# Scatter of an expert's rows as two float32r products with a one-hot matrix

## The chip, the cores and the metric

One core of a Trainium2 chip runs the whole program. The metric is the device time of one execution in microseconds (us); the time before is the median of three runs.

## The reference

The program computes two transformer blocks on 256 tokens of width 1024. The change touches only the second layer of the first block, a mixture of 8 experts (`moe_swiglu`). Each token goes to the 2 experts with the largest router logits, with softmax gates. Cut to what matters:

```python
top_logits, top_idx = lax.top_k(logits, TOP_K)        # 2 of 8
gates = jax.nn.softmax(top_logits, axis=-1)
...
h = jax.nn.silu(xb @ w1[e]) * (xb @ w3[e])            # 1024 -> 3584
y = h @ w2[e]                                         # 3584 -> 1024
y = y * gate_pad[:, None]
out = zeros.at[tok_pad].add(y)                        # back to the tokens' rows
```

## The kernel before

The experts run one after the other in a hardware loop (`turn`, once per expert, the last one outside the loop). At most 128 tokens of an expert are taken together (CAP = 128): a one-hot matrix gathers their rows, and another one scatters the result.

All weights are float32 in memory. Each 1 MB piece of weights (a slot, 128x2048) is loaded by two DMAs of 512 KB on the SP queue into a ring of 6 slots. ScalarE (ACT) copies it to float32r, the upper part (`weights_hi`, L1652), and VectorE (DVE) writes the rest as a second float32r tile (`weights_lo`, L1918). TensorE (PE) then forms a product as hi*hi + lo*hi + hi*lo, three float32r matmuls for each 128x512 block: L1158, L1159 and L1162 for w1 and w3 (`up_slot`), L1173, L1174 and L1178 for w2 (`down_slot`). A slot is 12 such matmuls, and a turn is 42 slots: 28 of "up" and 14 of "down". They run in the order up 1, down 0, up 2, down 1, up 3, down 2, next 0 (the first chunk of the next expert), down 3. At its slot s, the text of ACT and of DVE converts slot s + 3 first and then does the other work of slot s, so all work on an engine lies in the order of the text. A load may begin when PE has released the slot that stood in its place in the ring.

What surrounds the change, in the order of a turn:

- up 1, slot 4: `scatter(it, 0)` (L1141) writes the previous expert's rows for the first 128 tokens into PSUM banks 6 and 7, one matmul per bank of 512 columns. DVE adds both banks to `yacc` (`add`, L2271). Up 1, slot 6: `scatter(it, 1)` does the same for the other 128 tokens in the same banks, and so waits until both adds of the first part are done. The scatters of the last expert stand behind the loop. With 8 experts, there are 9 pairs, the first of them on zeros: 18 calls, 36 matmuls.
- down 1, slot 1: PE transposes `PG` (one-hot times gate, 128x256) into bank 6 (L1208), and ACT copies it to `PGT`, the stationary matrix of the scatter. PE waits for that copy at up 3, slot 1, where bank 6 is used again.
- down 3, slot 1, the last slot of a turn: ACT copies bank 4 and DVE copies bank 5 (L2318) to `Ysb`, the expert's 128x1024 result. ACT's copies of this kind all carry the line of a helper, L1466.
- at the head of the next turn, DVE does the lower part of the transposed activations (L2283), builds `PG` (`weigh`, L2256 to L2259) and the next gather matrix (`choose`, L2249 to L2252), converts four slots and then does the two adds of `scatter(it, 0)`.

Of the kernel before, what the change touches and what calls it, by code (L numbers as in the profile page):

```python
# [7 lines left out]
F32 = mybir.dt.float32  # L8
# [6 lines left out]
P = 128  # L15
# [15 lines left out]
CAP = P  # L31
# [218 lines left out]
def two_block_kernel(nc, a, out):  # L250

    CO, CONST_W = constant_offsets()
    with ExitStack() as ctx:
# [20 lines left out]
        def sem(name):  # L274

            if name not in S:
                S[name] = ctx.enter_context(nc.semaphore(name))
            return S[name]
# [111 lines left out]
        silu1 = ar(2, TT, FC)  # L390
        bufs1 = ffn_buffers(1, ar.at, silu1)
        ar.at += 3 * 4 * T
        Ysb = ar(D)
        Pm, PG, PGT = ar(TT, CAP), ar(TT, CAP), ar(TT, P)
        lo_slots = split_parts("weights_lo", "ring_data", 0, RING, 8 * FC)
        xT_hi, xT1_lo = split_parts("xT_hi", "actT", 0, DT, T), split_parts("xT_lo1", "arena", ar.at, DT, T)
        xg_hi, xg_lo = (split_parts(f"xg_{k}", "actT", D * i, DT, CAP) for i, k in enumerate(("hi", "lo")))
# [6 lines left out]
        fneg, fsum, frec = sm(H, TT), sm(H, TT), sm(H, TT)  # L404
        lgt, gtm, eqm = sm(TT, E), sm(TT, 64), sm(TT, 64)
        rank, sel, m1, ex, esum, gate = sm(TT, E), sm(TT, E), sm(TT), sm(TT, E), sm(TT), sm(TT, 2, E)
        posx, cnt, poscol, gcol = sm(TT, 2, E), sm(3), sm(TT), sm(TT)


        ring2 = Ring(ring_data, [sem(f"loaded2_{i}") for i in range(RING)], sem("weights2_used"), sem("weights2_hi"), sem("weights2_lo"), (2 * MIX_LOADS + FFN_LOADS) % RING)  # L410
# [394 lines left out]
        def _(pe):  # L805
# [308 lines left out]
            def moe():  # L1114
# [23 lines left out]
                def scatter(it, j):  # L1138

                    for q in range(2):  # L1140
                        mm(bank[6 + q][:, :], PGT[:, j, :], Ysb[:, 512 * q:512 * q + 512], start=True, stop=True).then_inc(sem("scatter_psum"), 1)  # L1141

                def turn_h(c):

# [36 lines left out]
                def turn(it, is_last):  # L1181
                    for s, (kind, c, m) in enumerate(Wide.slots(is_last)):
                        split = FFN_LOADS + e_first + s + 1 + it * MOE_LOADS
                        part = (kind, c, m)
                        if part in (("up", 1, 0), ("up", 2, 0), ("up", 3, 0), ("next", 0, 0)):

                            pe.wait_ge(sem("moe_h"), it * 4 + (c or 4))
                        if part == ("next", 0, 0):
                            pe.wait_ge(sem("xg_ready"), it + 2)
                        if part == ("up", 1, 1):  # L1190
                            turn_h(0)
                        if part == ("up", 1, 4):
                            pe.wait_ge(sem("ysb_ready"), it * 2 + 2)
                            pe.wait_ge(sem("pgT_ready"), it + 1)
                            pe.wait_ge(sem("moe_hT"), it * 4 + 1)
                            scatter(it, 0)
                        if part == ("up", 1, 6):
                            pe.wait_ge(sem("y_added"), it * 4 + 2)
                            scatter(it, 1)
                        if part == ("up", 2, 1):  # L1200
                            pe.wait_ge(sem("y_added"), it * 4 + 4)
                            turn_h(1)
                        if part == ("down", 1, 0):
                            pe.wait_ge(sem("moe_hT"), it * 4 + 2)
                        if part == ("down", 1, 1):
                            pe.wait_ge(sem("pg_ready"), it + 1)
                            for j in range(TT):
                                i = nc.tensor.transpose(bk(6, TT, P)[:, j], PG[:, j, :], ident)  # L1208
                            i.then_inc(sem("pgT_psum"), 1)
                        if part == ("up", 3, 1):  # L1210
                            pe.wait_ge(sem("pgT_ready"), it + 2)
                            turn_h(2)
                        if part == ("down", 2, 0):
                            pe.wait_ge(sem("moe_hT"), it * 4 + 3)
                            if not is_last:
                                gather(it + 1)
                        if part == ("next", 0, 1) or (is_last and part == ("down", 3, 0)):
                            if is_last:
                                pe.wait_ge(sem("moe_h"), it * 4 + 4)
                            turn_h(3)  # L1220
                        if part == ("down", 3, 0):
                            pe.wait_ge(sem("moe_hT"), it * 4 + 4)
                        (down_slot if kind == "down" else up_slot)(c, m, e_first + s, split)
# [240 lines left out]
        def _(act):  # L1464
            def a_(o, i, f, inc, **kw):
                nc.scalar.activation(o, i, f, **kw).then_inc(sem(inc), 1)  # L1466
# [187 lines left out]
            def moe():  # L1654
                act.wait_ge(sem("router_max"), 1)
                for j in range(TT):
                    a_(ex[:, j], lgt[:, j], ACT.Exp, "router_exp", bias=m1[:, j:j + 1])
                act.wait_ge(sem("npass_ready"), 1)
                last = act.value_load(npass_i[0:1, 1:2], min_val=E - 1, max_val=2 * E - 1)

                def gathered(it):
                    for b in range(2):
                        act.wait_ge(sem("gather_psum"), it * 2 + b + 1)
                        a_(xg_hi[:, 4 * b:4 * b + 4, :], bk(6 + b, 4, CAP), ACT.Copy, "xg_hi")

                def silu(c, used):
                    act.wait_ge(ring.used, used)
                    for q in range(Wide.WIDTHS[c] // 512):
                        i = nc.scalar.activation(esil[:, 512 * q:512 * q + 512], bank[q][:, :], ACT.Silu)
                    i.then_inc(sem("moe_silu"), 1)  # L1670

                def turned(c, n):
                    act.wait_ge(sem("moe_hT_psum"), n)
                    for b in range(Wide.WIDTHS[c] // 512):
                        i = nc.scalar.activation(ehT_hi[:, 4 * b:4 * b + 4, :], bk(6 + b, 4, P), ACT.Copy)
                    i.then_inc(sem("moe_hT_hi"), 1)

                def turn(it, is_last):
                    slots = Wide.slots(is_last)
                    n = len(slots)  # L1680
                    for s, (kind, c, m) in enumerate(slots):
                        if not is_last or s + Wide.LEAD < n:
                            e_high(e_first + s + Wide.LEAD, it)
                        used = n_moe + e_first + s + 1 + it * MOE_LOADS
                        part = (kind, c, m)
                        if part == ("up", 1, 0):
                            turned(0, it * 4 + 1)
                        if part == ("up", 2, 0):
                            turned(1, it * 4 + 2)
                        if part == ("down", 1, 1):  # L1690
                            act.wait_ge(sem("pgT_psum"), it + 1)
                            a_(PGT[:, :, :], bk(6, TT, P), ACT.Copy, "pgT_ready")
                        if part == ("up", 3, 0):
                            turned(2, it * 4 + 3)
                        if kind == "up" and m == Wide.UPS[c] - 1:
                            silu(c, used)
                            if c == 3 and not is_last:
                                gathered(it + 1)
                        if part == ("next", 0, 0) or (is_last and part == ("down", 2, 3)):
                            turned(3, it * 4 + 4)  # L1700
                        if part == ("next", 0, 7):
                            silu(0, used)
                        if part == ("down", 3, 1):
                            act.wait_ge(ring.used, used)
                            a_(Ysb[:, 0:512], bank[4][:, :], ACT.Copy, "ysb_ready")

                gathered(0)
                for m in range(2, e_first + Wide.LEAD):
                    if m == e_first + 1:
                        silu(0, n_moe + e_first)  # L1710
                    e_high(m)
                with act.Fori(0, last) as it:
                    turn(it, False)
                turn(last, True)
# [169 lines left out]
        def _(dve):  # L1884
# [316 lines left out]
            def moe():  # L2201
# [84 lines left out]
                def turn(it, is_last):  # L2286
                    slots = Wide.slots(is_last)
                    n = len(slots)
                    for s, (kind, c, m) in enumerate(slots):
# [23 lines left out]
                            turned_low(3, it * 4 + 4)  # L2313
                        if part == ("next", 0, 7):
                            multiply(0, it * 4 + 5)
                        if part == ("down", 3, 1):
                            dve.wait_ge(ring.used, n_moe + e_first + s + 1 + it * MOE_LOADS)
                            v.tensor_copy(Ysb[:, 512:1024], bank[5][:, :]).then_inc(sem("ysb_ready"), 1)  # L2318

                choose(0)  # L2320
                gathered(0)
                st.do(v.tensor_scalar(yacc[:, :, :], x[:, :, :], ALPHA, None, ALU.mult))

                v.memset(PGT[:, :, :], 0.0).then_inc(sem("pgT_ready"), 1)
                v.memset(Ysb[:, 0:512], 0.0).then_inc(sem("ysb_ready"), 1)
                v.memset(Ysb[:, 512:], 0.0).then_inc(sem("ysb_ready"), 1)
                st.settle()
                for m in range(2, e_first + Wide.LEAD):
                    if m == e_first + 1:
# [271 lines left out]
```

## Time and profile before

| | |
|---|---|
| three runs | 2479.80, 2483.47, 2486.38 us |
| median | 2483.47 us |
| span of the profiled execution, first to last instruction | 2475.4 us |
| busy: PE, DVE, ACT, POOL | 2313.0, 1569.0, 1140.9, 160.4 us |
| the expert loop with its ends, about 704 to 1738 us of the span | some 1034 us |
| one turn of the loop | 127.37 us |
| mean DMA rate over 740 to 1730 us | 345 GB/s |

The profiled execution has a span of 2475.4 us. Its own time is not listed apart; the median of the runs lies 8.1 us above the span and the lowest run 4.4 us, which is what lies around the span together with the spread between runs. Times in rows are us from the start of the span. PE's matmuls overlap in the records (each ends later than the next begins), so the distance from start to start tells what one costs.

### The profile page before, as it was taken

What the parts mean: (1) busy time and instruction counts of PE and PEld (TensorE: products, weight loads), DVE (VectorE), ACT (ScalarE), POOL (GpSimd) and SP (SyncE); (2) the same over time, 40 slices, a digit from 0 to 9 for tenths busy, and PEclk for the clock granted to TensorE, in tenths of its full rate; (3) what the DMA queues carried; (4) which work ended last, traced back from release to release, by engine and by line L of the source; (5) the groups of instructions that cost most, each with busy time, mean ns of one, the idle gap of its engine ahead of it and who ended that gap; (6) DMA issues with size and microseconds to landing.
All of it is one profiled execution on the core that took longest, in us unless ns stands there. A gap on an engine that the chain in (4) does not pass through costs nothing.

```text
span 2475.4 us, 31988 instructions
## 1 busy us (share of the span) xinstructions
PE 2313.0 (93%) x12191; PEld 1883.8 (76%) x12191; DVE 1569.0 (63%) x1677; ACT 1140.9 (46%) x1147; POOL 160.4 (6%) x224
## 2 busy tenths in 40 slices
PE   7987999798879999999999999999699999988997
PEld 6776788786767878787878787877588788756886
DVE  2565544365568888888898888887654219433443
ACT  1231443113246766667666666666544312222442
POOL 1010000102020000000000000000670001000000
PEclk9998999898889999999999999999899989788999
DMA  7402455450159999999999999999255444223552
GB/s 253 140 2 69 157 182 175 128 166 2 49 191 340 346 345 345 345 346 348 342 347 345 344 345 346 344 349 354 95 197 186 152 142 136 85 94 102 187 184 71
DMA packets 257660, 536.95 MB, mean 217 GB/s; under 512 B 20126, under 2 KB 150056, under 8 KB 257448
## 3 DMA queue, kind: packets, MB, share of 16 engines
q1 hardware_dynamic: 251088, 523.21, 60.1%
q0 software_dynamic: 3168, 9.86, 1.2%
q10 hardware_dynamic: 3320, 2.72, 0.3%
q8 instruction: 58, 0.95, 0.2%
q14 instruction: 26, 0.21, 0.0%
HBM read 532.57 MB, written 3.15 MB: 216 GB/s over the span
## 4 chain that ended last, share of the span: by engine, by line
PE 90%; DVE 5%; ACT 2%; issue 1%; ACTq 1%; DMA 0%; DVEq 0%; POOL 0%
PE bank L1159 8%; PE bank L1158 8%; PE bank L1162 8%; PE bank L1053 8%; PE bank L1054 8%; PE bank L1055 7%; PE bank L861 5%; PE bank L1292 4%; PE bank L1178 4%; PE bank L1173 4%; PE bank L1174 4%; PE bank L1030 2%; PE bank L857 1%; PE bank L1135 1%; PE bank L1141 1%
## 5 line engine op out<-in xcount | busy, mean ns | idle before, releaser
L1918 DVE TENSOR_TENSOR weights_lo<-ring_data,weights_hi 128x2048 fp32r<-128x2048 f32 x336 | 759.6, 2289 | 100.2 <-ACT weights_hi L1652 99.0
L1652 ACT ACTIVATE weights_hi<-ring_data 128x2048 fp32r<-128x2048 f32 x336 | 635.6, 1917 | 181.1 <-DMA ring_data<-in_moe_w 180.1
L1158 PE MATMUL bank<-weights_hi,xg_hi 128*128 128x512 f32 x896 | 363.4, 406 | 4.0 <-DVE arena L2277 2.6
L1159 PE MATMUL bank<-weights_hi,xg_lo 128*128 128x512 f32 x896 | 354.6, 396 | 0.0
L1913 DVE TENSOR_TENSOR weights_lo<-ring_data,weights_hi 128x2048 fp32r<-128x2048 f32 x99 | 229.7, 2348 | 51.7 <-ACT weights_hi L1491 51.7
L1466 ACT ACTIVATE arena<-bank 128x512 f32<-128x512 f32 (+4 forms) x178 | 83.6, 488 | 371.0 <-PE bank L861 111.8
L1162 PE MATMUL bank<-weights_lo,xg_hi 128*128 128x512 f32 x896 | 243.0, 393 | 0.0
L1053 PE MATMUL bank<-weights_hi,xT_hi 128*128 128x512 f32 x528 | 214.4, 406 | 16.3 <-issue 16.3
L1054 PE MATMUL bank<-weights_lo,xT_hi 128*128 128x512 f32 x528 | 210.9, 399 | 0.0
L1055 PE MATMUL bank<-weights_hi,xT_lo 128*128 128x512 f32 x528 | 210.6, 399 | 0.0
L1158 PEld LDWEIGHTS bank<-weights_hi,xg_hi 128*128 128x128 f32 x896 | 168.2, 188 | 46.1 <-issue 6.8
L1159 PEld LDWEIGHTS bank<-weights_hi,xg_lo 128*128 128x128 f32 x896 | 168.7, 188 | 42.0 <-issue 3.8
L1162 PEld LDWEIGHTS bank<-weights_lo,xg_hi 128*128 128x128 f32 x896 | 168.3, 188 | 40.2
L1491 ACT ACTIVATE weights_hi<-ring_data 128x2048 fp32r<-128x2048 f32 x99 | 185.7, 1917 | 0.0
L1173 PE MATMUL bank<-weights_hi,hT_hi 128*128 128x512 f32 x448 | 177.7, 397 | 1.5 <-DVE hT_lo L2283 1.5
L1174 PE MATMUL bank<-weights_hi,hT_lo 128*128 128x512 f32 x448 | 175.7, 392 | 0.0
L1930 DVE TENSOR_TENSOR hT_lo<-bank,hT_hi 128x256 fp32r<-128x256 f32 x66 | 25.0, 420 | 174.5 <-ACT hT_hi L1502 174.5
L861 PE MATMUL bank<-actT,ring_data 128*128 128x256 f32 x608 | 131.6, 379 | 0.0
L1053 PEld LDWEIGHTS bank<-weights_hi,xT_hi 128*128 128x128 f32 x528 | 101.0, 191 | 40.0 <-issue 17.4
L861 PEld LDWEIGHTS bank<-actT,ring_data 128*128 128x128 f32 x608 | 115.5, 190 | 15.6
L1502 ACT ACTIVATE hT_hi<-bank 128x256 fp32r<-128x256 f32 x66 | 21.7, 381 | 225.2 <-PE bank L1074 225.2
L1178 PE MATMUL bank<-weights_lo,hT_hi 128*128 128x512 f32 x448 | 123.1, 396 | 0.0
(432 smaller groups left out, 3261.0 us busy)
## 6 DMA issues: line engine op xcount, KB each, us to landing
ring_data<-in_moe_w SPq DMA_DIRECT2D x672, 512.0 KB, 4.2
ring_data<-in_ffn_w_in SPq DMA_DIRECT2D x88, 512.0 KB, 4.7
ring_data<-in_w_in SPq DMA_DIRECT2D x70, 512.0 KB, 4.7
ring_data<-in_ffn_w SPq DMA_DIRECT2D x66, 512.0 KB, 4.0
ring_data<-in_ffn_w_out SPq DMA_DIRECT2D x44, 512.0 KB, 3.9
ring_data<-in_w_out SPq DMA_DIRECT2D x24, 512.0 KB, 4.2
ring_data<-in_w_in SPq DMA_DIRECT2D x8, 396.0 KB, 4.0
ring_data<-in_w_in SPq DMA_DIRECT2D x8, 390.0 KB, 6.7
```

Source lines behind the costliest of these rows:

```text
L861: i = mm(bk(b, 2, T)[:, t], wt[:, k, P * t:P * t + P], actT[:, k, :], start=k == 0, stop=k == DT - 1)
L1053: mm(o, x_hi, w_hi, start=start, stop=False, **kw)
L1054: mm(o, x_hi, w_lo, start=False, stop=False, **kw)
L1055: return mm(o, x_lo, w_hi, start=False, stop=stop, **kw)
L1158: mm(o, xg_hi[:, k, :], e_hi(at)[:, r], start=k == 0, stop=False)
L1159: mm(o, xg_lo[:, k, :], e_hi(at)[:, r], start=False, stop=False)
L1162: i = mm(bank[2 * part + q][:, :], xg_hi[:, k, :], e_lo(at)[:, r], start=False, stop=k == DT - 1)
L1173: mm(o, ehT_hi[:, 2 * m + f, :], w_hi[:, f, cd], start=first and f == 0, stop=False)
L1174: mm(o, ehT_lo[:, 2 * m + f, :], w_hi[:, f, cd], start=False, stop=False)
L1652: nc.scalar.activation(e_hi(at), ring_data[:, e_slot(at), :], ACT.Copy).then_inc(ring.hi_done, 1)
L1913: v.tensor_tensor(f.lo_slot(f.n0 + at), w, f.hi_slot(f.n0 + at), ALU.subtract).then_inc(f.ring.lo_done, 1)
L1918: v.tensor_tensor(e_lo(at), ring_data[:, e_slot(at), :], e_hi(at), ALU.subtract).then_inc(ring.lo_done, 1)
```

## The change

The float32 matrix `PGT` (one-hot times gate) is split into a matrix of zeros and ones, `chosen` in float32r, and the gate of each of the 128 rows, `gslot`, which ACT gets as the row sum of its copy (`accum_out`). The gated result is held as two float32r parts: `Y_hi`, both halves by ACT straight from banks 4 and 5 with the gate as scale, and `Y_lo`, by DVE as bank*gate - `Y_hi`. Each scatter matmul becomes two, `chosen` times `Y_hi` and `chosen` times `Y_lo`, accumulated in one bank. DVE makes `chosen` with a comparison. PE has one more wait (`gslot_ready`), DVE waits for `y_hi`, and one of the memsets ahead of the loop is larger. The number of bytes loaded is the same.

```diff
 def scatter(it, j):
     for q in range(2):
-        mm(bank[6 + q][:, :], PGT[:, j, :], Ysb[:, 512 * q:512 * q + 512], start=True, stop=True).then_inc(sem("scatter_psum"), 1)
+        r = slice(512 * q, 512 * q + 512)
+        mm(bank[6 + q][:, :], chosen[:, j, :], Y_hi[:, r], start=True, stop=False)
+        mm(bank[6 + q][:, :], chosen[:, j, :], Y_lo[:, r], start=False, stop=True).then_inc(sem("scatter_psum"), 1)
...
 if part == ("up", 3, 1):                              # PE
     pe.wait_ge(sem("pgT_ready"), it + 2)
+    pe.wait_ge(sem("gslot_ready"), it + 1)
...
 if part == ("down", 1, 1):                            # ACT
     act.wait_ge(sem("pgT_psum"), it + 1)
-    a_(PGT[:, :, :], bk(6, TT, P), ACT.Copy, "pgT_ready")
+    a_(gate_row[:, :, :], bk(6, TT, P), ACT.Copy, "gslot_ready", accum_out=gslot[:, 0:1])
...
 if part == ("down", 3, 1):                            # ACT
     act.wait_ge(ring.used, used)
-    a_(Ysb[:, 0:512], bank[4][:, :], ACT.Copy, "ysb_ready")
+    act.wait_ge(sem("gslot_ready"), it + 1)
+    for q in range(2):
+        a_(Y_hi[:, 512 * q:512 * q + 512], bank[4 + q][:, :], ACT.Copy, "y_hi", scale=gslot[:, 0:1])
...
+if part == ("down", 1, 1):                            # DVE
+    dve.wait_ge(sem("gslot_ready"), it + 1)
+    v.tensor_scalar(chosen[:, :, :], gate_row[:, :, :], 0.0, None, ALU.is_gt).then_inc(sem("pgT_ready"), 1)
 if part == ("down", 3, 1):                            # DVE
-    dve.wait_ge(ring.used, n_moe + e_first + s + 1 + it * MOE_LOADS)
-    v.tensor_copy(Ysb[:, 512:1024], bank[5][:, :]).then_inc(sem("ysb_ready"), 1)
+    for q in range(2):
+        r = slice(512 * q, 512 * q + 512)
+        dve.wait_ge(sem("y_hi"), it * 2 + q + 1)
+        v.scalar_tensor_tensor(Y_lo[:, r], bank[4 + q][:, :], gslot[:, 0:1], Y_hi[:, r], ALU.mult, ALU.subtract).then_inc(sem("ysb_ready"), 1)
...
-v.memset(PGT[:, :, :], 0.0).then_inc(sem("pgT_ready"), 1)
-v.memset(Ysb[:, 0:512], 0.0).then_inc(sem("ysb_ready"), 1)
-v.memset(Ysb[:, 512:], 0.0).then_inc(sem("ysb_ready"), 1)
+v.memset(chosen.bitcast(F32)[:, :, :], 0.0).then_inc(sem("pgT_ready"), 1)
+v.memset(Y_hi.bitcast(F32)[:, :], 0.0).then_inc(sem("ysb_ready"), 1)
+v.memset(Y_lo.bitcast(F32)[:, :], 0.0).then_inc(sem("ysb_ready"), 1)
```

## Rows read from the trace of the kernel before

**Rows 1.** The page, busy time and share of the span by engine.
```profile
PE 2313.0 (93%) x12191; PEld 1883.8 (76%) x12191; DVE 1569.0 (63%) x1677; ACT 1140.9 (46%) x1147; POOL 160.4 (6%) x224
```
**Rows 2.** Busy time of each engine in a stretch of one turn.
```profile
core 0: us, PE busy (x) PEld busy (x) DVE busy (x) ACT busy (x) POOL busy (x), PEclk, DMA share, GB/s
...
880.00:1008.00 128.00, 128.00 (x578) 103.34 (x577) 109.85 (x71) 88.47 (x61) 0.00 (x0) 1.00 0.94 345
```
**Rows 3.** PE in order of time around a scatter: start, length, line.
```profile
1002.65 1.09 PE L1162 MATMUL bank<-weights_lo,xg_hi 128*128 128x512 f32 x4
1003.57 1.88 PE L1141 MATMUL bank<-arena 128*128 128x512 f32 x4
...
1005.52 0.39 PE L1159 MATMUL bank<-weights_hi,xg_lo 128*128 128x512 f32 x1
...
1010.85 1.88 PE L1141 MATMUL bank<-arena 128*128 128x512 f32 x4
```
**Rows 4.** All scatter matmuls: least, median and greatest ns.
```profile
L1141 PE MATMUL bank<-arena x72: 591/592/697, 748.4 to 1736.7; 128*128 128x512 f32 x72
```
**Rows 5.** DVE in order of time, from a turn's end to the adds.
```profile
993.52 0.68 DVE L2318 COPY arena<-bank 128x512 f32<-128x512 f32 x1
994.18 2.29 DVE L1918 TENSOR_TENSOR weights_lo<-ring_data,weights_hi 128x2048 fp32r<-128x2048 f32 x1
...
999.16 8.89 DVE L1918 TENSOR_TENSOR weights_lo<-ring_data,weights_hi 128x2048 fp32r<-128x2048 f32 x4
1007.97 1.28 DVE L2271 TENSOR_TENSOR arena<-arena,bank 128x512 f32<-128x512 f32 x2
...
1136.07 1.28 DVE L2271 TENSOR_TENSOR arena<-arena,bank 128x512 f32<-128x512 f32 x2
```
**Rows 6.** ACT in order of time at the same turn's end.
```profile
991.75 0.60 ACT L1466 ACTIVATE arena<-bank 128x512 f32<-128x512 f32 x1 [0.79 <-PE bank L1178]
992.24 1.91 ACT L1652 ACTIVATE weights_hi<-ring_data 128x2048 fp32r<-128x2048 f32 x1
```
**Rows 7.** Groups by shape whose operations are nearest to the new ones.
```profile
L1466 ACT ACTIVATE xT_hi<-bank,pcol 128x256 fp32r<-128x256 f32 x16 | 6.0, 489 | 7.0 <-PE bank L820 7.0
...
L1466 ACT ACTIVATE arena<-bank 128x256 f32<-128x256 f32 x17 | 6.3, 380 | 31.3 <-PE bank L861 18.3 <-PE bank L1288 10.0 <-PE bank L1292 3.0
...
L1906 DVE SCALAR_TENSOR_TENSOR xT_lo<-bank,pcol,xT_hi 128x256 fp32r<-128x256 f32 x16 | 6.5, 476 | 1.8 <-PE bank L820 1.8
...
L2547 DVE SCALAR_TENSOR_TENSOR x<-bank,x 128x512 f32<-128x512 f32 x8 | 5.0, 684 | 11.9 <-PE bank L1055 11.9
...
L2453 DVE TENSOR_SCALAR arena<-arena 128x384 f32<-128x384 f32 x1 | 0.4, 361 | 0.0
```
**Rows 8.** DVE behind the memsets, and PE at the first turn's second scatter.
```profile
727.52 2.29 DVE L1918 TENSOR_TENSOR weights_lo<-ring_data,weights_hi 128x2048 fp32r<-128x2048 f32 x1 [0.80 <-ACT weights_hi L1652]
...
756.01 1.98 PE L1141 MATMUL bank<-arena 128*128 128x512 f32 x4 [0.19 <-DVE arena L2271]
```
**Rows 9.** The last expert's scatters behind the loop, in order of time.
```profile
1731.81 0.69 DVE L2318 COPY arena<-bank 128x512 f32<-128x512 f32 x1 [6.00 <-PE bank L1178]
...
1732.56 1.99 PE L1141 MATMUL bank<-arena 128*128 128x512 f32 x4 [0.78 <-DVE arena L2318]
...
1733.72 0.69 DVE L2271 TENSOR_TENSOR arena<-arena,bank 128x512 f32<-128x512 f32 x1 [1.22 <-PE bank L1141]
...
1737.35 0.69 DVE L2271 TENSOR_TENSOR arena<-arena,bank 128x512 f32<-128x512 f32 x1 [0.17 <-PE bank L1141]
```
**Rows 10.** DMA over 740 to 1730 us in 40 slices; times to landing.
```profile
GB/s 291 350 387 305 373 332 345 371 305 369 348 337 363 314 363 360 330 359 328 349 369 319 362 361 319 360 321 371 353 317 374 310 370 360 315 368 319 362 375 333
...
DMA to landing us min/median/max: 3.1/4.2/6.3
```
**Rows 11.** What the DMA queue waited for, 880 to 1008 us.
```profile
SPq L595 <- PE bank L1162: 53.8, 28, 3.4
SPq L595 <- PE bank L1178: 27.7, 14, 5.3
```

More of the change, by code:

```diff
@@ L392, in two_block_kernel @@
         ar.at += 3 * 4 * T
-        Ysb = ar(D)
-        Pm, PG, PGT = ar(TT, CAP), ar(TT, CAP), ar(TT, P)
+        at_Y = ar.at
+        Y_hi = split_parts("Y_hi", "arena", ar.at, D)
+        Y_lo = split_parts("Y_lo", "cln", 0, D)
+        ar.at += D
+        Pm, PG, gate_row = ar(TT, CAP), ar(TT, CAP), ar(TT, P)
+        at_chosen = ar.at
+        chosen = split_parts("chosen", "arena", ar.at, TT, P)
+        ar.at += TT * P
         lo_slots = split_parts("weights_lo", "ring_data", 0, RING, 8 * FC)
@@ L406, in two_block_kernel @@
         rank, sel, m1, ex, esum, gate = sm(TT, E), sm(TT, E), sm(TT), sm(TT, E), sm(TT), sm(TT, 2, E)
-        posx, cnt, poscol, gcol = sm(TT, 2, E), sm(3), sm(TT), sm(TT)
+        posx, cnt, poscol, gcol, gslot = sm(TT, 2, E), sm(3), sm(TT), sm(TT), sm(1)
         ring2 = Ring(ring_data, [sem(f"loaded2_{i}") for i in range(RING)], sem("weights2_used"), sem("weights2_hi"), sem("weights2_lo"), (2 * MIX_LOADS + FFN_LOADS) % RING)
```

## The prediction

> **What bounds the kernel now.** I read the page first. PE is busy for 2313.0 of 2475.4 us, and no other engine comes near [rows 1]. The share is a mean over stages, so the next view is that of the expert loop alone, where the change lies. In a stretch of one turn PE is busy for 128.00 of 128.00 us at the full granted clock (2.4 GHz), DVE for 109.85 and ACT for 88.47 [rows 2]. The reader should see that there is no gap at all on PE: what PE is spared here shortens the turn, as long as nobody else comes too late. Two others could. DVE is at 86%, and the DMA engines at 94% [rows 2]. So I then read the timeline of DVE and ACT where the change adds work to them, and the DMA views. The DMA queue itself spends 53.8 + 27.7 = 81.5 of 128 us waiting for PE to release a slot [rows 11]: loads follow PE, they do not lead it.
>
> **The scatter on PE.** Before, one call is 2 float32 products. The trace keeps two records for each (72 for 36) [rows 4]. From the first start to the next product with weights is 1005.52 - 1003.57 = 1.95 us, and one float32r product (the L1158 that lies between) must come off. Four float32r products take 1003.57 - 1002.65 = 0.92 us, so one is 0.23 and the call is 1.72 us [rows 3]. After, one call is 4 float32r products with weights loaded for each, just what L1162 does: 0.92 to 0.93 us. A call gets 1.72 - 0.93 = 0.79 us shorter, and the 18 calls, all on the path, would give 14.2 us. That is the upper bound; now the calls are taken one kind at a time.
>
> **The seven later turns.** Two calls each: 2 x 0.79 = 1.58 us, 11.1 us for seven, if nothing waits. The place where something could wait is `scatter(it, 1)`, which needs both adds of `scatter(it, 0)`. DVE ends these adds at 1007.97 + 1.28 = 1009.25, and PE starts the call at 1010.85 [rows 3, 5]: 1.60 us of slack. The change eats it from both ends. First, PE comes 0.79 us earlier because `scatter(it, 0)` is shorter. Second, DVE comes later. Its copy L2318 (0.68) becomes two operations that read a bank, a column and a tile. The nearest rows are the same operation on 128x256 with a column (476 ns, 6.5 / 16 = 0.41 us of busy time each) and on 128x512 with a constant (684 ns) [rows 7]. A 128x512 one with a column should be 0.69 to 0.75, the pair 1.41, so DVE is 0.73 us later. From 994.18 DVE works almost without a gap up to the adds, four conversions in 8.89 us among it [rows 5], so nothing there absorbs the delay. What is left is 1.60 - 0.79 - 0.73 = 0.08 us. It is just enough on paper; with 0.1 us of error in each term I allow a mean wait of 0.1 us in each turn, 0.7 us in all. In one turn the adds start at 1136.07, 0.73 us later than 1007.97 + 127.37 = 1135.34 [rows 5], because ACT's conversion came late; there the new DVE work falls into DVE's idle time, and the slack is again about 0.08.
>
> DVE must not wait for ACT before `Y_lo`. ACT starts its copy at 991.75, when the bank is complete [rows 6]. A 128x512 copy takes 0.60 there; a scale column costs 489 - 380 = 109 ns more on 128x256 [rows 7], so 0.71, and two of them end by about 991.75 + 1.3 = 993.05. DVE reaches this point at 993.52 [rows 5], later, so it does not wait. ACT's next conversion moves from 992.24 to 992.9 and ends at 994.8; DVE needs it after its own two operations, at 993.52 + 1.41 = 994.93. This hides the ACT part too, by 0.1 us only. If that cover is gone, each tenth goes to the same 0.08 us of slack.
>
> **The other edits in a turn.** `chosen` is a comparison on 128x256 from SBUF; the nearest row is 361 ns on 128x384 [rows 7], so about 0.3 us. It stands behind a conversion in the middle of the turn, four slots (4 x 12 x 0.23, 11 us) before PE asks for it, and DVE has 128 - 110 = 18 us of idle time in the turn, none of it needed by PE [rows 2]. The row sum adds a short read to ACT's copy in the same place; even at a whole extra copy (0.38 us, [rows 7]) it is under the same cover. PE's extra wait is for something done long before. I put all three at nothing, with an upper bound of 0.7 us on the two engines but not on PE.
>
> **The first turn and the memsets.** Here `scatter(0, 1)` starts at 756.01 after waiting 0.19 us for DVE's adds [rows 8]. DVE is itself late at this point, so a faster `scatter(0, 0)` only makes PE wait 0.98 instead of 0.19: gain 0. The second call still gives 0.79. The larger memset costs DVE about 1 us, but DVE waits for ACT 0.80 us at 727.52 [rows 8] and stands idle again after that conversion. Nothing.
>
> **Behind the loop.** Now the change is a chain with no cover. Before: bank complete at 1731.81, copy 0.69, PE at 1732.56, first add at 1733.72 (1.16 later), last add ends at 1737.35 + 0.69 = 1738.04: 6.23 us [rows 9]. After: first `Y_hi` 0.71, second by 1.3, then DVE's two from 0.75 to 2.16, PE at 2.2. The first sum is ready one product earlier than before: a pair takes 0.46 where the float32 product took 0.86, so 1.16 becomes 0.76. Then two adds, 1.35, and the second call repeats both: 2.2 + 2 x (0.76 + 1.35 + 0.05) = 6.5 us. A loss of 0.3 us, between 0 and 0.6.
>
> **The sum.** 11.1 - 0.7 + 0.8 - 0.3 = 10.9, say 11 us. All later stages begin after the loop and move with it; their loads are issued as slots come free. The span would be 2475.4 - 11 = 2464.4 us. The median of the runs is 8.1 us above the span, and I carry the difference over: 2483.5 - 11 = 2472.5 us. Bounds: 14 if every call counted; 5.5 if the whole gain of `scatter(it, 0)` were lost to DVE in seven turns.
>
> **DMA against a rule.** A turn loads 42 x 1.049 = 44.0 MB, now at 345 GB/s; in 125.8 us it would be 350 GB/s. One slice of 24.75 us already shows 387 GB/s, several over 370 [rows 10], so the trace leaves room. The Trainium skill, "HBM Reference", Specifications, gives an effective 358 GB/s per core, and in Access says a core alone streams well above it. By the 358 a turn could not be shorter than 44.0 / 0.358 = 123 us, still under 125.8, and the sum would be the same; the slices over 358 side with its second statement.
>
> **Rivals.**
>
> *A, as above: PE sets the turn.* 2472.5 us. For it: no gap on PE. Range of its own 2469 to 2476. Chance 0.68.
>
> *B, DVE comes too late for `scatter(it, 1)`.* The slack of 0.08 us is small against the sum of three estimates. If DVE is 0.8 us later than I think, seven turns lose 5.6 us and the gain is 5.3: 2478 us. It needs a slower column operation or a wait for the second `Y_hi`; against it speak the rows of the same operation. Chance 0.15.
>
> *C, the loads cannot come faster.* If 345 GB/s is all that this pattern yields, PE will wait for weights what it is spared: 2483 us. For it: the share of 94% in the turn. Against: the queue's 81.5 us of waiting for PE, and slices of 370 to 387 GB/s; time to landing is at most 6.3 us where PE takes 5 x 2.79 = 14 us to come round to the slot. Chance 0.09.
>
> *D, slower.* `Y_hi` stands on ACT behind a conversion that waits for its load, and DVE now waits for ACT before it may go on, which it did not before. If that load is late by L, DVE's conversions and the adds are late by L less the cover: 0.79 us of idle ACT [rows 6], 0.47 between 993.05 and 993.52, 0.08 of slack. Each us beyond 1.3 costs a us in each of seven turns. At L = 2.9 the gain of 11 is gone; at L = 4.5 the kernel is at about 2483.5 - 11 + 7 x 3.2 = 2495 us. The greatest landing time is only 2.1 us above the median [rows 10], so it would have to be a new kind of lateness. Chance 0.04. The remaining 0.04 is for more than 14 us of gain, from a change of the loads' timing that I do not see.
>
> **How the numbers follow.** The bound between a change and none is 0.3%, 7.5 us, about the spread of these runs: 2476.0 is where "faster" begins. A lies 3.5 us beyond it. A and the rest of 0.04 make 0.72; I leave a little of A to "same" for the spread of a median of three. Same: B, C and that, 0.26. Slower: D, 0.04. The range reaches from 2467 (14 us of gain and some spread) to 2481 (B and some spread), and leaves out C and D.
>
> **What the profile after would show.** L1141's successor as four float32r products in 0.93 us; turns of 127.37 - 1.58 = 125.8 us, plus what PE waits at `scatter(it, 1)`; the adds of `scatter(it, 0)` ending 5.68 + 0.73 = 6.4 us after its start (now 1009.25 - 1003.57 = 5.68); DVE's idle time before `Y_lo` near 0 with ACT as releaser only behind the loop; the DMA rate in a turn at 350 GB/s. PE idle time with DVE's add as its releaser, 0.5 us or more in each turn, would speak for B; idle time with `weights_hi` or `weights_lo` for C; DVE idle before `Y_lo` for D. The prediction is wrong if a float32r product that follows another on the same bank costs more than 0.23 us, or if DVE's gapless run in front of the adds is longer than I count.

## The result

| | median | runs | span of the profiled execution |
|---|---|---|---|
| before | 2481.64 us | 2478.05 to 2486.38, 4 runs | 2475.4 us |
| after | 2465.75 us | 2462.36 to 2469.73, 4 runs | 2466.9 us |

The ratio of the runs is 0.9940, with a 95% interval from 0.9924 to 0.9955: the kernel became faster, by 0.45 to 0.76%. The forecast was 2472.5 us with a range from 2467 to 2481. The direction was right; the measured median lies 1.25 us below the range.

The two profiled executions differ by only 8.5 us, although the medians differ by 15.9. The four runs after took 2469.73, 2464.70, 2466.80 and 2462.36 us, and the profiled one is the slowest of them, with a span of 2466.9: only 2.8 us lie around the span. This disagreement between profile and clock is the first thing to be explained; the second is whether the steps of the sum were right.

### The profile page after: what moved, and what is told of

It is laid out like the page before. It is cut to its first block, busy times and chain, and to the rows that moved or that the text cites. A ratio compares the mean times of both kernels' runs of the same rounds, so it can differ in the third digit from the quotient of the medians.

```text
span 2466.9 us, 32044 instructions
## 1 busy us (share of the span) xinstructions
PE 2303.1 (93%) x12191; PEld 1886.1 (76%) x12191; DVE 1575.4 (64%) x1693; ACT 1147.8 (47%) x1163; POOL 160.3 (6%) x224
## 4 chain that ended last, share of the span: by engine, by line
PE 89%; DVE 6%; ACT 2%; issue 2%; ACTq 1%; DMA 1%; DVEq 0%; POOL 0%; SPq 0%
PE bank L1167 8%; PE bank L1166 8%; PE bank L1170 8%; PE bank L1059 8%; PE bank L1060 8%; PE bank L1061 8%; PE bank L867 5%; PE bank L1301 4%; PE bank L1186 4%; PE bank L1181 4%; PE bank L1182 4%; PE bank L1036 2%; PE bank L863 1%; PE bank L1141 1%; PE bank L1449 1%
## 5 line engine op out<-in xcount | busy, mean ns | idle before, releaser
L1166 PE MATMUL bank<-weights_hi,xg_hi 128*128 128x512 f32 x896 | 357.0, 398 | 4.0 <-DVE arena L2288 2.6
```

What stands on the lines that cost most here:

```text
L1166: mm(o, xg_hi[:, k, :], e_hi(at)[:, r], start=k == 0, stop=False)
```

## The profile after

The page and a window of two turns, as in [rows 1] and [rows 2]:

```profile
PE 2303.1 (93%) x12191; PEld 1886.1 (76%) x12191; DVE 1575.4 (64%) x1693; ACT 1147.8 (47%) x1163; POOL 160.3 (6%) x224
```

```profile
877.28:1003.04 125.76, 125.76 (x575) 102.78 (x574) 109.93 (x72) 89.07 (x63) 0.00 (x0) 1.00 0.96 350
1003.04:1128.82 125.78, 125.78 (x576) 102.74 (x574) 110.12 (x72) 89.21 (x63) 0.00 (x0) 1.00 0.95 350
```

These stretches reach from one `scatter(it, 0)` to the next. A turn is 125.76 us, where it was 127.37: 1.61 us less, forecast 1.58. PE is still busy without a gap at the full clock, and the DMA rate is 350 GB/s, as worked out. The Trainium skill's 358 GB/s for a core ("HBM Reference", Specifications) bound nothing here; the turn stays below it, and single slices had gone over it already [rows 10]. The Trainium skill's sentence on a core that streams alone, which the prediction puts under Access, stands under Specifications as well.

PE and DVE in order of time around the scatter, to set beside [rows 3] and [rows 5]:

```profile
1002.81 0.40 PE L1170 MATMUL bank<-weights_lo,xg_hi 128*128 128x512 f32 x1
1003.04 0.39 PE L1148 MATMUL bank<-Y_hi,chosen 128*128 128x512 f32 x1
1003.27 0.39 PE L1149 MATMUL bank<-Y_lo,chosen 128*128 128x512 f32 x1
1003.50 0.39 PE L1148 MATMUL bank<-Y_hi,chosen 128*128 128x512 f32 x1
1003.73 0.39 PE L1149 MATMUL bank<-Y_lo,chosen 128*128 128x512 f32 x1
1003.96 0.40 PE L1166 MATMUL bank<-weights_hi,xg_hi 128*128 128x512 f32 x1
...
1009.54 0.40 PE L1148 MATMUL bank<-Y_hi,chosen 128*128 128x512 f32 x1
```

```profile
993.00 1.40 DVE L2334 SCALAR_TENSOR_TENSOR Y_lo<-bank,small,Y_hi 128x512 fp32r<-128x512 f32 x2
994.42 2.29 DVE L1929 TENSOR_TENSOR weights_lo<-ring_data,weights_hi 128x2048 fp32r<-128x2048 f32 x1
...
999.25 8.89 DVE L1929 TENSOR_TENSOR weights_lo<-ring_data,weights_hi 128x2048 fp32r<-128x2048 f32 x4
1008.06 1.28 DVE L2282 TENSOR_TENSOR arena<-arena,bank 128x512 f32<-128x512 f32 x2
```

A call is 1003.96 - 1003.04 = 0.92 us, four products 0.23 apart, where it was 1.72. DVE enters `Y_lo` without idle time, and its adds end at 1008.06 + 1.28 = 1009.34. PE comes back at 1009.54. The slack of 1.60 us has shrunk to 0.20 (forecast 0.08): present, and nearly used up. PE came 0.78 us earlier, counted from the first call (6.50 us instead of 7.28), and DVE's adds started 0.62 us later (5.02 us after the first call instead of 4.40), where 0.73 had been forecast.

The new operations by shape, beside [rows 7]:

```profile
L2334 DVE SCALAR_TENSOR_TENSOR Y_lo<-bank,small,Y_hi 128x512 fp32r<-128x512 f32 x16 | 11.2, 745 | 6.7 <-ACT Y_hi L1475 6.7
...
L1475 ACT ACTIVATE Y_hi<-bank,small 128x512 fp32r<-128x512 f32 x16 | 10.1, 685 | 12.6 <-PE bank L1186 12.6
...
L2329 DVE TENSOR_SCALAR chosen<-arena 128x256 fp32r<-128x256 f32 x8 | 2.3, 286 | 0.0
```

All three fall where the nearest rows had put them (0.69 to 0.75, 0.71 and 0.3 us). DVE waits for `Y_hi` 6.7 us in all, and that is the wait behind the loop alone, where ACT itself waits as long for PE's last bank.

Two places stand apart from these turns. At the first turn's second call PE waits for DVE, 0.97 us where 0.98 had been forecast:

```profile
757.91 0.50 PE L1148 MATMUL bank<-Y_hi,chosen 128*128 128x512 f32 x1 [0.97 <-DVE arena L2282]
```

Behind the loop it went otherwise than in the sum. Beside [rows 9], all engines in order of time:

```profile
1721.63 1.27 ACT L1475 ACTIVATE Y_hi<-bank,small 128x512 fp32r<-128x512 f32 x2 [6.73 <-PE bank L1186]
1722.35 1.41 DVE L2334 SCALAR_TENSOR_TENSOR Y_lo<-bank,small,Y_hi 128x512 fp32r<-128x512 f32 x2 [6.72 <-ACT Y_hi L1475]
...
1723.82 0.80 PE L1148 MATMUL bank<-Y_hi,chosen 128*128 128x512 f32 x1 [2.22 <-DVE Y_lo L2334]
1724.41 0.63 PE L1149 MATMUL bank<-Y_lo,chosen 128*128 128x512 f32 x1
1724.83 0.63 PE L1148 MATMUL bank<-Y_hi,chosen 128*128 128x512 f32 x1
...
1728.79 0.69 DVE L2282 TENSOR_TENSOR arena<-arena,bank 128x512 f32<-128x512 f32 x1 [0.17 <-PE bank L1149]
```

From the last bank complete (ACT starts at 1721.63) to the end of the last add (1728.79 + 0.69 = 1729.48) are 7.85 us. It was 6.23; the forecast was 6.5. The copies end as worked out: PE starts 2.19 us after the bank is complete, forecast 2.2. But the products then stand 0.42 us apart and not 0.23. The windows give the clock that PE was granted there, first after, then at the second call behind the loop in the kernel before:

```profile
1718.00:1721.00 3.00, 3.00 (x15) 2.42 (x14) 0.00 (x0) 0.00 (x0) 0.00 (x0) 1.00 1.09 350
1721.00:1724.00 3.00, 0.78 (x4) 0.34 (x3) 1.41 (x2) 2.37 (x3) 0.00 (x0) 0.92 0.99 349
1724.00:1726.00 2.00, 1.89 (x4) 0.98 (x4) 0.76 (x2) 2.00 (x2) 0.00 (x0) 0.50 1.05 349
```

```profile
1734.60:1738.00 3.40, 2.18 (x5) 0.81 (x5) 2.01 (x3) 2.69 (x2) 0.00 (x0) 1.00 0.59 201
```

A granted clock of 0.50 is 1.2 GHz, where 1.00 is 2.4.

To compare the loop between executions, I use the time from the first scatter's first record to the end of the last add. Before it is 748.37 to 1738.04, 989.67 us; after it is 750.28 to 1729.48, 979.20 us. So the loop with its ends gained 10.5 us, and the stages ahead of it took 1.9 us more in this one profile. The rest, behind the last add, is 737.4 us in both.

## The experiments

### Both kernels again

No edit; both kernels were timed and profiled again.

> The changed kernel as it is, timed again. Theory 1 (all of the gain lies in the expert loop): between the first scatter and the last add the profiles show 989.67 us before and 979.20 after, so 10.5 us, and the rest of the 15.9 us between the medians is the spread of the runs: ratio 0.9958, 10 to 12 us. Theory 2 (the stages ahead of the loop gain too): 15 us again, ratio 0.994, and a profile in which the loop begins earlier than at 748.37 us, the place before. In both the turns take 125.76 us.

> The kernel before, timed against itself, as a measure of the spread. Theory 1: ratio 1.000 with an interval of some 0.001 to each side; single runs 2478 to 2487 us, and the first scatter starts within 2 us of 748.37 us while turns take 127.37 us again. Theory 2: the start of the loop is the same within 0.5 us in each profile of this kernel.

The changed kernel took 2469.28 us (2465.61 to 2471.72, 6 runs) and is at 0.9955 of the kernel before (0.9941 to 0.9969), 11.2 us; the medians are 12.8 us apart (2482.08 before, 23 runs). The kernel before against itself is at 0.9998 (0.9987 to 1.0009), with a median of 2480.91; its single runs reach from 2474.27 to 2487.67, further down than the 2478 expected. PE of the changed kernel and of the kernel before, in order of time, first call and the same call a turn later:

```profile
749.25 0.39 PE L1148 MATMUL bank<-Y_hi,chosen 128*128 128x512 f32 x1
...
755.74 0.39 PE L1148 MATMUL bank<-Y_hi,chosen 128*128 128x512 f32 x1
...
875.01 0.39 PE L1148 MATMUL bank<-Y_hi,chosen 128*128 128x512 f32 x1
```

```profile
752.31 1.88 PE L1141 MATMUL bank<-arena 128*128 128x512 f32 x4
...
879.69 1.88 PE L1141 MATMUL bank<-arena 128*128 128x512 f32 x4
```

The kernel before began its loop at 748.37 in one execution and at 752.31 in the other, so theory 2's condition (the same within 0.5 us) fell, and so did theory 1's (within 2 us). Over all eleven profiles of this study the start lies between 747.02 and 754.87 us, in kernels whose work ahead of the loop is the same but for the memsets, and without order by kernel. (Two memsets are larger in the changed kernel, not one: 0.91 us each instead of 0.48.) Behind the last add come 736.6 to 741.7 us. The loop itself repeats: 989.67 and 989.20 us before, 979.20 and 977.62 after. The difference of 1.6 between the last two comes from the first turn (127.00 and 125.76 us), where PE waited 0.97 us in the first profile and not at all in this one (755.74), and from the end (7.85 and 7.55 us).

So the loop gains between 10.0 and 12.1 us, the second timing agrees, and over the eleven profiles the start of the loop moves by some 8 us and the stretch behind it by some 5, whatever the kernel. The first comparison, with four runs to a side, showed 15.9 us between medians, and its interval begins at 11.2.

The kept traces say something on where the start of the loop is lost. A window of 25 us ahead of it, in the second profile of the changed kernel (loop from 749.25) and of the kernel before (from 752.31):

```profile
125.00:150.00 25.00, 22.02 (x108) 16.12 (x106) 18.58 (x25) 10.10 (x32) 0.00 (x0) 0.90 0.00 1
125.00:150.00 25.00, 22.38 (x93) 15.92 (x91) 18.17 (x24) 7.51 (x29) 0.00 (x0) 0.80 0.00 0
```

In the seven profiles whose loop begins before 751 us the granted clock is 0.90 to 1.00 here, and ACT reaches its table load at the end of this stretch at 147.86 to 148.78. In the four that begin after 752 it is 0.80 or 0.67, and the same table load comes at 150.48 to 153.41. No weights are loaded in this window, so the loads are not behind it. The table load is late by 1.7 to 5.5 us, the start of the loop by 2.0 to 7.9. The clock and the lateness go together; no run changed one of them, so that the clock is the cause is not shown.

### New parts, old product

```diff
-mm(bank[6 + q][:, :], chosen[:, j, :], Y_hi[:, r], start=True, stop=False)
-mm(bank[6 + q][:, :], chosen[:, j, :], Y_lo[:, r], start=False, stop=True).then_inc(...)
+mm(bank[6 + q][:, :], chosen.bitcast(F32)[:, j, :], Y_hi.bitcast(F32)[:, r], start=True, stop=True).then_inc(...)
```

> The changed kernel with the old price on TensorE: one float32 product of chosen with Y_hi for each bank, Y_lo is computed but left out of the scatter. Theory 1: a turn takes 127.37 us again, since VectorE still ends its adds before TensorE comes back (1.60 - 0.73 = 0.87 us of slack); only the end behind the loop is longer, by 1.5 us. Time: before + 1.5 us, ratio 1.0006. Rival (the gain comes from the new elementwise work, or that work costs the loop something): a turn away from 127.37 us by more than 0.1 us.

Measured: 1.0013 (0.9999 to 1.0028). PE in order of time:

```profile
1009.61 1.88 PE L1148 MATMUL bank<-Y_hi,chosen 128*128 128x512 f32 x4
...
1136.99 1.88 PE L1148 MATMUL bank<-Y_hi,chosen 128*128 128x512 f32 x4
...
1740.08 2.51 PE L1148 MATMUL bank<-Y_hi,chosen 128*128 128x512 f32 x4 [2.22 <-DVE Y_lo L2333]
1743.37 3.78 PE L1148 MATMUL bank<-Y_hi,chosen 128*128 128x512 f32 x4 [0.78 <-DVE arena L2281]
```

A turn is 1136.99 - 1009.61 = 127.38 us again. The whole gain of a turn is the product's price, and the elementwise work costs a turn nothing. The end behind the loop takes 9.99 us (1737.89 to 1747.88), 3.8 more than before and not 1.5: four records that took 1.98 us now take 2.51 in the first call and 3.78 in the second, at a granted clock of 0.50. My expectation missed that. The ratio cannot tell 3.8 us from 1.5: both lie in its interval.

### Only the upper part; one operation more on DVE; the gather matrix later

Three runs to measure the slack at `scatter(it, 1)`. They were timed once each, so only their turns are compared. The edits, cut to what matters:

```diff
 # only the upper part (one product per bank)
-mm(bank[6 + q][:, :], chosen[:, j, :], Y_hi[:, r], start=True, stop=False)
-mm(bank[6 + q][:, :], chosen[:, j, :], Y_lo[:, r], start=False, stop=True).then_inc(...)
+mm(bank[6 + q][:, :], chosen[:, j, :], Y_hi[:, r], start=True, stop=True).then_inc(...)
...
 # one more: DVE, down 3, slot 1, ahead of the first Y_lo
+v.tensor_copy(spare, bank[4][:, :])
...
 # one more and choose later: DVE, with the copy too
 if part == ("up", 1, 4):
     add(it, 0)
+    if not is_last:
+        choose(it + 1)          # taken out of up 1, slot 0
```

> The changed kernel with one float32r product for each bank, chosen with Y_hi; Y_lo is computed but left out of the scatter. A call takes 0.46 us on TensorE instead of 0.93. Theory (VectorE's adds are the next thing to be late, with 0.20 us of slack now): in each of the seven turns TensorE waits 0.26 us for the add before the second call, and a turn takes 125.76 - 0.93 + 0.26 = 125.1 us. Rival (slack is larger than the trace says): 124.83 us without a wait.

> The changed kernel with one more VectorE copy (128x512 from bank 4 into an unused tile) ahead of the first Y_lo in each turn. Theory (0.20 us of slack at the second call, VectorE without a gap up to it): the adds come 0.67 us later, TensorE waits 0.47 us in each of seven turns, a turn takes 126.2 us, 3.3 us more over the loop. Rival (the delay is absorbed on the way): 125.76 us a turn.

> As the run with one more copy on VectorE, but the next gather matrix is built after the adds of the first call instead of before the four conversions. Theory (what counts is VectorE's work between the end of a turn and the adds): about 0.8 us is taken out of that stretch, the adds end 0.1 us or more before those of the changed kernel, no wait of TensorE, a turn 125.76 us. Rival (VectorE's total load counts): 126.2 us as in the run without the move.

PE with only the upper part, both calls of one turn and the first of the next:

```profile
1006.59 0.62 PE L1148 MATMUL bank<-Y_hi,chosen 128*128 128x512 f32 x2
...
1012.84 0.73 PE L1148 MATMUL bank<-Y_hi,chosen 128*128 128x512 f32 x2
...
1131.77 0.62 PE L1148 MATMUL bank<-Y_hi,chosen 128*128 128x512 f32 x2
```

1131.77 - 1006.59 = 125.18 us, where the theory said 125.1 and the rival 124.83. The second call comes 6.25 us after the first, 0.22 later than the 6.49 - 0.46 = 6.03 that it would be without a wait. PE with one copy more:

```profile
999.02 0.39 PE L1149 MATMUL bank<-Y_hi,chosen 128*128 128x512 f32 x1
...
1005.85 0.50 PE L1149 MATMUL bank<-Y_hi,chosen 128*128 128x512 f32 x1 [0.17 <-DVE arena L2283]
...
1125.22 0.39 PE L1149 MATMUL bank<-Y_hi,chosen 128*128 128x512 f32 x1
```

126.20 us, forecast 126.2. The bracket names only 0.17 us of idle PE, because a matmul's modelled end lies later than the start of the next one could; from start to start the call comes 6.83 us after the first one, where it is 6.49 or 6.50 without a wait, and the first product of the call then costs 0.11 us more. With the gather matrix built later (and the copy still there), the first calls of two turns:

```profile
999.83 0.39 PE L1149 MATMUL bank<-Y_hi,chosen 128*128 128x512 f32 x1
...
1125.59 0.39 PE L1149 MATMUL bank<-Y_hi,chosen 128*128 128x512 f32 x1
```

That is 125.76 us. So the slack that the forecast worked out is shown from both sides: it is about 0.2 us. One copy more on DVE between the end of a turn and the adds (0.68 us) costs a turn 0.44 us, what it is beyond the slack, and with other work of about that size moved behind the adds it costs nothing.

### A warm end and a short end

The warm end was timed once, so only its profile is read.

```diff
 turn(last, True)                                       # PE, warm end
+for _ in range(8):
+    mm(bank[0][:, :], xg_hi[:, 0, :], xg_hi[:, 0:4, :], start=True, stop=True)
 pe.wait_ge(sem("ysb_ready"), last * 2 + 4)
```

```diff
 turn(last, True)                                       # PE, short end
+for q in range(2):
+    pe.wait_ge(sem("ysb_ready"), last * 2 + 3 + q)
+    r = slice(512 * q, 512 * q + 512)
+    for j in range(TT):
+        o = bank[(6, 0)[j] + q][:, :]
+        mm(o, chosen[:, j, :], Y_hi[:, r], start=True, stop=False)
+        mm(o, chosen[:, j, :], Y_lo[:, r], start=False, stop=True).then_inc(sem("scatter_psum"), 1)
...                                                     # DVE's adds in the same order
```

> The changed kernel with eight idle float32r products into bank 0 behind the loop, while TensorE would wait for Y_lo; their result is used by nobody. In the changed kernel the granted clock there is 0.50 and scatter products come 0.42 us apart. Theory (the clock falls because TensorE stands idle for 2.2 us behind an idle of 1.5 us): clock 1.00, products 0.23 us apart, and the last add ends about 7.86 - 1.2 = 6.6 us after the last bank is complete. Rival (the products are slow there because they follow a wait): 7.86 us again.

> The changed kernel; behind the loop the two halves of the result are scattered as each Y_lo is ready, into four banks (6, 7, 0, 1) so that no product waits for an add. From the last bank complete to the last add it is 7.86 us in the changed kernel. Theory (a chain of copy, lower part, product, adds, each waiting): first Y_hi 0.7, first Y_lo 1.5, first sum about 2.4, then VectorE is the bound with one more Y_lo and four adds, 5.0 to 5.4 us: 2.5 to 2.9 us less than the changed kernel, ratio to before about 0.9947 if that of the changed kernel is 0.9958. Rival (the layer norm behind it waits for something else): no change of the time.

The warm end, windows over its last stretches and PE there:

```profile
1721.00:1723.00 2.00, 1.81 (x8) 1.13 (x6) 1.27 (x2) 1.99 (x3) 0.00 (x0) 1.00 0.84 289
1723.00:1725.00 2.00, 1.20 (x4) 0.68 (x4) 1.17 (x3) 2.00 (x2) 0.00 (x0) 1.00 1.01 329
```

```profile
1720.81 2.01 PE L1242 MATMUL bank<-xg_hi 128*128 128x512 f32 x8
1723.20 0.50 PE L1148 MATMUL bank<-Y_hi,chosen 128*128 128x512 f32 x1 [0.38 <-DVE Y_lo L2336]
1723.53 0.40 PE L1149 MATMUL bank<-Y_lo,chosen 128*128 128x512 f32 x1
1723.77 0.39 PE L1148 MATMUL bank<-Y_hi,chosen 128*128 128x512 f32 x1
```

The clock stays at 1.00, the products stand 0.23 us apart, and the end takes 6.35 us (1721.01 to 1727.36) instead of 7.85. The sum had said 6.5. What the idle PE had cost there is 1.5 us against the first profile of the changed kernel and 1.2 against the second (7.55). The Trainium skill, "TensorE: Matmul & The Clock Gate", What's actually happening, has TensorE throttled by default and its full clock released by activity; the trace agrees, 0.50 after the idle times and 1.00 where filler products took their place.

The same profile shows something that I had not looked for. Its loop is that of the changed kernel, yet one of its seven later turns has a wait before the second call (PE, both calls of that turn and the first of the next):

```profile
1127.62 0.39 PE L1148 MATMUL bank<-Y_hi,chosen 128*128 128x512 f32 x1
...
1134.60 0.50 PE L1148 MATMUL bank<-Y_hi,chosen 128*128 128x512 f32 x1 [0.32 <-DVE arena L2284]
...
1253.97 0.39 PE L1148 MATMUL bank<-Y_hi,chosen 128*128 128x512 f32 x1
```

The second call comes 6.98 us after the first instead of 6.49, and the turn takes 126.35 us. Ahead of that turn a conversion on ACT had waited 1.90 us for its load (at 1106.02), where the two before it had waited 1.2, and DVE, 1.52 us idle for it, came to `Y_lo` 9.31 us ahead of the first call instead of 10.05 a turn earlier. By this trace a late load is enough to use up a slack of 0.20 us: it happened in one of 28 turns, counting the four profiles with this loop code.

The short end, DVE in order of time:

```profile
1720.39 1.41 DVE L2337 SCALAR_TENSOR_TENSOR Y_lo<-bank,small,Y_hi 128x512 fp32r<-128x512 f32 x2 [6.72 <-ACT Y_hi L1478]
1721.96 2.48 DVE L2358 TENSOR_TENSOR arena<-arena,bank 128x512 f32<-128x512 f32 x4 [0.16 <-PE bank L1247]
```

From 1719.67 to 1724.44 are 4.77 us, 3.1 or 2.8 less than in the two profiles of the changed kernel; I had expected 5.0 to 5.4. Part of this is the clock, which stays at 1.00 here, and part the shorter chain. DVE works from its first `Y_lo` to the last add with 0.16 us of idle time, and PE's products are 0.23 us apart after an idle time of 1.56 us. Loop with ends 974.85 us (749.59 to 1724.44). Behind the last add come 737.56 us, as with the changed kernel (737.4 and 738.6), so the rival, a layer norm that waits for something else, finds no support. Timed: 0.9945 (0.9931 to 0.9959) of the kernel before, median 2465.96 us.

### Both edits together

> The changed kernel with both edits that shortened something: the halves scattered as they are ready, into four banks, behind the loop, and the next gather matrix built after the adds of the first call. Theory 1 (the loop with its ends is all that differs): turns of 125.76 us, no wait of TensorE before the second call of the first turn (it was 0.97 us in one profile of the changed kernel and 0 in another), 4.77 us behind the loop; from the first scatter to the last add 974.5 to 975 us, 14.5 us less than before, ratio 0.994. Theory 2 (moving the gather matrix frees something in every turn): turns below 125.7 us.

From 754.66 to 1729.52 are 974.86 us, no wait in the first turn, turns of 125.76 us (880.42 to 1006.18), and 4.78 us behind the loop. So theory 1 holds: 14.3 to 14.8 us less than the kernel before in the loop, and moving the gather matrix freed nothing, since PE already set the turn. It did widen the slack: DVE ends the adds at 1011.77 and PE comes back at 1012.67, 0.90 us instead of 0.20, more than the late turn above would have needed; no run shows such a turn with the move. That PE does not wait in the first turn proves nothing for the move, as it did not wait in the short end without it either. Timed: 0.9949 (0.9931 to 0.9966), 2468.05 us; this execution's loop began at 754.66, late in the range of 747.0 to 754.9. The profiles separate both short versions from the changed kernel by 2.8 to 4.3 us in the loop, but the timings do not: 0.9945, 0.9949 and 0.9955 lie within one another's intervals.

## Why the prediction was right in its steps and missed the time

- *PE sets the turn.* Right: 100% busy before and after, 125.76 us a turn against 125.8 forecast, and with the old product 127.38 again.
- *The price of a call.* Right: 1.72 and 0.92 us (forecast 0.93).
- *The slack at `scatter(it, 1)`.* Right in kind and within 0.12 us: 0.20, forecast 0.08. The 0.7 us that I had put in for waits in the seven turns did not come in the two profiles of the changed kernel; in the profile of the warm end, with the same loop code, 0.6 us did. Rival B was near: one copy more on DVE costs 0.44 us a turn, over half of the 0.8 that it supposed.
- *`chosen`, the row sum, PE's wait.* Cost nothing in a turn, shown by the run with the old product.
- *The first turn.* The forecast wait was there in the changed kernel's first profile (0.97 us) and absent in the second. Half right: DVE starts its adds 6.30 us after the first call in one execution and 4.90 in the other, and the sum had only the first case.
- *Behind the loop.* The mechanism (a chain without cover) was right, the term mis-sized: a loss of 0.3 us forecast, 1.6 and 1.3 measured. The cause was left out of the sum: the granted clock fell to 0.50 behind PE's idle time of 2.2 us in front of the products. The warm end, where idle products fill that time and the clock stays at 1.00, shows it.
- *Rivals C and D.* C would have kept the turn at 127.37 us; the loads came at 350 GB/s. D did not occur as told: DVE never waited for `Y_hi` inside the loop. But a late load did delay DVE once, by the 0.7 us seen in the warm end's profile.

The sum of 10.9 us met 10.5 in the first pair of profiles, 11.6 in the second and 11.2 in the second timing. In part that is luck: the 0.7 us for waits that did not come made up for the end that was 1.0 to 1.3 us worse than forecast.

The step that failed is in "How the numbers follow": the size of the spread. The range took a gain of 14 us and only 2.5 us more for spread, around a base of 2483.5 us that was itself the median of three runs. The miss of 6.75 us (2472.5 forecast, 2465.75 measured) has two parts. The base was 1.8 us too high: the kernel before came out at 2481.64 in the same comparison, and at 2482.08 and 2480.91 in the second timing. The other 4.9 us are the distance between the 15.9 us of the first medians and the 11 of the sum, and most of them did not come back: the second timing shows 11.2 us (12.8 between medians). The same changed kernel took 2469.28 us there, inside the range, and all ten runs of it together have a median of 2467.87. So the first median fell below the range by the draw of its four runs; a median inside so narrow a margin would have been luck as well. Single runs of the kernel before spread over 13 us (2474.27 to 2487.67), and a median of three of the 23 runs in the second timing lies, by my estimate from all such triples, anywhere between 2476.3 and 2487.7 in 95 of 100 cases. The start of the loop alone differs by 3.9 us between the two profiles of the kernel before.

"The sum" had the warning in hand. Carrying 8.1 us from span to median changes nothing in it, since 2464.4 + 8.1 is the same as 2483.5 - 11. But a run's time is its own span plus 1.8 to 2.9 us, so the profiled execution of the kernel before had taken about 2478 us, less than any of the three runs shown: most of the 8.1 us was spread and not a constant. What makes the stages ahead of the loop vary stays open; the granted clock in them goes with it, as shown above, and no run changed it.

## What to carry to other kernels

When an engine is busy without a gap over a loop, cheaper instructions on it come back one to one, up to the first wait whose slack they use; work out that slack from both sides, the engine that comes earlier and the one that comes later. The work that hides in a loop stands uncovered behind it: there, make the chain short, start each half as soon as it is ready, and use banks that nobody needs any more. A slack read from one turn is a slack without a late load; one turn in 28 had less. Before giving a range, compare the span of the profiled run with that run's own time, and let the range hold the spread of a median.

## What the runs showed of the hardware

- In six profiles with 2.2 or 2.8 us of idle TensorE ahead of the last scatters the granted clock fell to 0.50 during them, not always at the same product: in the run with the gather matrix later, after 2.8 us, the first call still stood 0.23 us apart. With 0.78 us of idle time (before) or 1.56 us (the short end) it stayed at 1.00 to the last product. A float32r product is 0.23 us at 1.00 and 0.42 at 0.50, and four records of float32 products take 1.98 and 3.78 us.
- A float32r product that adds to a bank just written by the one before costs the same 0.23 us as one into another bank.
- A float32 product of 512 columns costs 0.86 us at 1.00, as much as 3.7 float32r products; two float32r parts with a matrix of zeros and ones cost 0.46.
